# Fifteen activation transposes moved from TensorE to the DMA queue in an eight-core hybrid decoder step

## What is computed

```
h   = rms_norm(x) * (1 + scale1) + shift1          # first norm
p   = h @ W_in                                     # seven column blocks of 512: q, f, i, g, B, C, h
mix = [HGRN2 recurrence over (q, f, i) * silu(g),  B * conv3(C * h)]
x   = x + gate1 * (mix @ W_out)
h2  = rms_norm(x) * (1 + scale2) + shift2          # second norm
x   = x + gate2 * (relu(h2 @ W_up)^2 @ W_down)     # the channel mixer
y   = rms_norm(x) * g_final
```

## Time and profile before

| | us |
|---|---|
| three timed runs | 858.78, 861.19, 865.7 (median 861.19) |
| the profiled execution | 858.85 |
| its span, first to last instruction | 857.3 |
| spans of the eight cores | 854.6 to 857.3 |
| TensorE busy | 810.3 |
| VectorE, ScalarE, POOL busy | 454.1, 369.2, 173.1 |

### The profile page before, as it was taken

One profiled execution on the slowest core, in us unless ns is written; L12 is line 12 of the kernel. 1 busy time (PEld: TensorE's weight loads), 2 busy tenths in 40 slices (PEclk: granted clock), 3 DMA queues, 4 the chain that ended last, 5 costly groups with the idle time before them and its releaser, 6 DMA issues.

```text
span 857.3 us, 16496 instructions; the slowest of 8 cores (854.6 to 857.3 us)
## 1 busy us (share of the span) xinstructions
PE 810.3 (95%) x5917; PEld 512.2 (60%) x5917; DVE 454.1 (53%) x876; ACT 369.2 (43%) x803; POOL 173.1 (20%) x231
## 2 busy tenths in 40 slices
PE   1479999999999999999999999999999999999996
PEld 1348876586876868656545654564456445644864
DVE  2366997377777867953015553455345535541522
ACT  3267963364676778447303322332233213310412
POOL 3110143353324231510003011101110111111002
PEclk9989999999999999999999999999999999999998
DMA  8999935988893349599995325212421432112001
GB/s 151 191 193 189 198 99 95 209 208 175 197 222 129 125 146 153 149 174 192 188 198 184 112 56 160 99 50 62 151 96 50 78 107 75 38 37 99 26 1 50
DMA packets 38957, 109.57 MB, mean 128 GB/s; under 512 B 15030, under 2 KB 16054, under 8 KB 33884
## 3 DMA queue, kind: packets, MB, share of 16 engines
q0 software_dynamic: 6624, 44.14, 31.1%
q1 hardware_dynamic: 30524, 58.34, 22.1%
q10 hardware_dynamic: 1728, 6.03, 2.2%
HBM read 123.93 MB, written 22.68 MB: 171 GB/s over the span
## 4 chain that ended last, share of the span: by engine, by line
PE 83%; DMA 11%; DVE 2%; issue 2%; ACT 1%; POOL 1%; DVEq 0%; ACTq 0%; POOLq 0%; SPq 0%
PE B L510 82%; DMA gates<-xr 4%; DMA win<-w_in 3%; DMA xe<-xp 3%; PE B L521 1%; ACT W L537 1%; DMA xn<-xp 1%; DMA xr<-xs 1%; POOL xr L544 0%; DVE Sd L544 0%; POOL mix L544 0%; DVE W L554 0%; DVE sg L554 0%; DVE ub L544 0%; DVE W L544 0%
## 5 line engine op out<-in xcount | busy, mean ns | idle before, releaser
L510 PE MATMUL B<-h2T,wup 128*128 128x384 bf16 (+1 forms) x1536 | 240.2, 317 | 0.0
L510 PE MATMUL B<-wdn,uT 128*128 128x512 bf16 (+1 forms) x1120 | 235.9, 373 | 0.0
L510 PE MATMUL B<-hT,win 128*128 128x256 bf16 (+1 forms) x1728 | 194.3, 269 | 6.1 <-DMA win<-w_in 5.4
L510 PEld LDWEIGHTS B<-h2T,wup 128*128 128x128 bf16 x1536 | 149.5, 98 | 83.8
L537 ACT ACTIVATE W<-B 128x384 f32<-128x384 f32 (+2 forms) x209 | 103.6, 497 | 204.3 <-PE B L510 187.3
L510 PEld LDWEIGHTS B<-wdn,uT 128*128 128x128 bf16 x1120 | 109.6, 98 | 124.8
L510 PEld LDWEIGHTS B<-hT,win 128*128 128x128 bf16 x1728 | 158.9, 99 | 27.9 <-issue 7.1
L544 POOL TENSOR_TENSOR xr<-xr,W 128x512 f32<-128x512 f32 x63 | 82.3, 1312 | 291.8 <-DVE W L544 256.3
L544 DVE TENSOR_TENSOR uT<-W,B 128x384 bf16<-128x384 f32 (+1 forms) x160 | 83.8, 525 | 80.5 <-ACT W L537 74.8
L544 DVE TENSOR_TENSOR W<-B,Gp 128x512 f32<-128x512 f32 (+1 forms) x65 | 44.2, 680 | 152.9 <-PE B L510 152.7
L537 ACT ACTIVATE W<-xr 128x1024 bf16<-128x1024 f32 (+2 forms) x19 | 18.3, 965 | 131.5 <-POOL xr L544 126.8
(11 more groups left out here) (157 smaller groups left out, 660.9 us busy)
## 6 DMA issues: line engine op xcount, KB each, us to landing
x<-xr SPq DMA_DIRECT2D x17, 512.0 KB, 10.6
xn<-x SPq DMA_DIRECT2D x17, 512.0 KB, 5.8
xr<-x SPq DMA_DIRECT2D x17, 512.0 KB, 4.1
ada<-w_ada POOLq DMA_DIRECT2D x8, 1024.0 KB, 14.7
xr<-xp SPq DMA_DIRECT2D x16, 512.0 KB, 10.0
wup<-w_up POOLq DMA_DIRECT2D x8, 1024.0 KB, 13.7
wdn<-w_down POOLq DMA_DIRECT2D x8, 1024.0 KB, 39.7
yp<-xr SPq DMA_DIRECT2D x15, 512.0 KB, 2.6
```

Source lines behind the costliest of these rows:

```text
L510: ins = e.matmul(o_, lhsT=l_, rhs=r_, start=st, stop=sp_, skip_group_check=True)
```

## The change

Three kinds of block turn from `tr` to `turn`: the first norm of prompt tiles 4 to 7 (two blocks each), both norms of the sample tile (`sample_mod`: its first norm, and its block in group 0), and the second norms of the prompt blocks of groups 0 and 1. That is 8 + 2 + 5 = 15 blocks; prompt tiles 0 to 3 keep TensorE's transposes. In each, scale and shift are then applied in place. The semaphore of a DMA is now keyed by the part of a buffer that it writes as well, so that two transposes into one operand are waited for apart.

```
-            key = eng + ((":in:" + writes[0][0].name) if (writes and (writes[0][0].rng is not None or not reads)) else (":out:" + reads[0][0].name))
+            key = eng + ((":in:" + writes[0][0].name + writes[0][1]) if (writes and (writes[0][0].rng is not None or not reads)) else (":out:" + reads[0][0].name))
...
     def sample_mod(nbv, nbn, dst, dst_n, c0, j_sh, j_sc, spare=None):
-        M, Mn = NR.take()
-        Mb = M[:, :].bitcast(BF16)
-        tr([(Mb[:, j * 128:(j + 1) * 128], nbv[:, j * 128:(j + 1) * 128], ident) for j in range(8)], [nbn, "cB"], [Mn])
+        turn(dst[:, :, c0:c0 + 128], nbv, [nbn], [dst_n + "#d0"], 128 * 2048)
...
-            tt("dve", tmv, trv, scb, ALU.mult, [Mn, "modT%d#%d" % (j_sc // 8, jh)], [Wn])
+            tt("dve", tmv, hv, scb, ALU.mult, [dst_n + "#d0", "modT%d#%d" % (j_sc // 8, jh)], [Wn])
...
     def norm1(kind, ti, eng="act"):
+        if ti >= 4:
+            for b in range(2):
+                turn(h[:, :, b * 128:(b + 1) * 128], nbs[b][0], [nbs[b][1]], ["%s#d%d" % (hn, b)], 128 * 2048)
+            for jj in range(8):
+                ts("dve", h[:, jj, :], h[:, jj, :], modT[:, 8 + jj, 0:1], modT[:, jj, 0:1], ALU.mult, ALU.add,
+                   [hn + "#d0", hn + "#d1", "modT0#%d" % (jj // 4), "modT1#%d" % (jj // 4)], ["%s#%d" % (hn, jj)])
+            return h, hn
...
-                norm2(bgroups[0][n_ - 5:n_ - 4], None, "h2T0_", n_ - 5)
+                norm2(bgroups[0][n_ - 5:n_ - 4], None, "h2T0_", n_ - 5, cross=True)
...
-            norm2(bgroups[1], h2T, "h2T", 0, got)
+            norm2(bgroups[1], h2T, "h2T", 0, got, cross=True)
```

More of the change, by code:

```diff
@@ L879, in sample_mod @@
     def sample_mod(nbv, nbn, dst, dst_n, c0, j_sh, j_sc, spare=None):
-        M, Mn = NR.take()
-        Mb = M[:, :].bitcast(BF16)
-        tr([(Mb[:, j * 128:(j + 1) * 128], nbv[:, j * 128:(j + 1) * 128], ident) for j in range(8)], [nbn, "cB"], [Mn])
+        turn(dst[:, :, c0:c0 + 128], nbv, [nbn], [dst_n + "#d0"], 128 * 2048)
         for jh in range(2):
             W, Wn = (spare[0][:, jh * 512:(jh + 1) * 512], "%s#%d" % (spare[1], jh)) if spare else WT.take()
-            trv = Mb[:, jh * 512:(jh + 1) * 512].rearrange("p (j s t) -> p j s t", s=16, t=8)
             tmv = W[:].rearrange("p (j s t) -> p j s t", s=16, t=8)
@@ L889, in sample_mod @@
             shb = AP(modT, (j_sh + 4 * jh) * 17 + 1, [[544, 128], [17, 4], [1, 16], [0, 8]])
-            tt("dve", tmv, trv, scb, ALU.mult, [Mn, "modT%d#%d" % (j_sc // 8, jh)], [Wn])
-            tt("dve", hv, tmv, shb, ALU.add, [Wn, "modT%d#%d" % (j_sh // 8, jh)], ["%s#%d" % (dst_n, jh)])
+            tt("dve", tmv, hv, scb, ALU.mult, [dst_n + "#d0", "modT%d#%d" % (j_sc // 8, jh)], [Wn])
+            tt("dve", hv, tmv, shb, ALU.add, [Wn, dst_n + "#d0", "modT%d#%d" % (j_sh // 8, jh)], ["%s#%d" % (dst_n, jh)])
     def norm1(kind, ti, eng="act"):
@@ L1226, in norm2 @@
                 hn = pre + "%d" % s
-                turn(dst, nbv, [nbn], [hn], 128 * 2048)
+                turn(dst, nbv, [nbn], [hn + "#d0"], 128 * 2048)
                 for j in range(8):
                     ts("dve", dst[:, j, :], dst[:, j, :], modT[:, 24 + j, 0:1], modT[:, 16 + j, 0:1], ALU.mult, ALU.add,
-                       ["%s#%d" % (hn, j), "modT2#%d" % (j // 4), "modT3#%d" % (j // 4)], ["%s#%d" % (hn, j)])
+                       [hn + "#d0", "modT2#%d" % (j // 4), "modT3#%d" % (j // 4)], ["%s#%d" % (hn, j)])
                 continue
```

## The result

The changed kernel took 900.86, 900.87 and 904.46 us, the kernel before 858.78 to 865.7 in the same series (four executions, median 861.8): ratio of the means 1.0465, 95% interval 1.0404 to 1.0526. It is slower, by 40 us, and outside the predicted range.

The account below looks back on a forecast made before the run. TensorE was taken as the bound, almost without idle time from 130 us on. Terms: -6.7 + 2 + 0.5 + 1.5 = -2.7 us, from a median of 861.19 to 858.5 us; range 852.3 to 873.

Parts of the forecast that it names:

- the price of tile 4's pair: Prompt tile 4: two transposes behind SP's earlier load land late, sm0 waits behind them; TensorE stall 0 to 8 us, taken 2.
- the top of a landing: Transposing DMA beside weights: up to 7.5 us taken, from kS and vS loads; ends kept at 1.3 and 58 us.
- The slower rival: Small packets take single turns beside weights, so stalls reach their upper ends: +13.4 us, 874.6 us; chance 0.21.
- the prediction's estimate: Transposes beside weights: by the skill page's 9 to 17 descriptors a packet, 62 descriptors make 4 to 7 turns, 4 to 7 us.
- the removed 6.7 us: TensorE, fifteen normed blocks: eight transposes each, 0.45 us a block, leave a stretch without slack; -6.7 us.
- zero for w_down and for PSUM: Group 0's `down`: 6.4 us of room covers 3.9 us later weights; PSUM: no wait for a bank shows; both zero.
- the other two stalls: Tile 5's second transpose behind convs: 0 to 3.3 us, taken 0.5; group 1's `up`, third transpose behind Gs: 0 to 8.8, taken 1.5.
- SP's own time: SP's queue: issuing fifteen transposes at 1.26 us, 19 us spread over 270 us of mostly waiting; counted as zero.
- Median landing 4 to 10 us; above 20 us the slower rival holds: Profile test on the first fifteen transposes' landings: median 4 to 10 us expected, above 20 us means packets take single turns.
- The warning on ScalarE's squares: ScalarE's next square into W0 or W1 waits until a transpose has landed; named as a possible unforeseen wait, no size given.

Follow-up runs that it names:

- the first experiment: Changed kernel with prompt tile 4's two blocks back on TensorE's transposes, the other thirteen by DMA; engine lists also reordered: 910.37 us, ratio 1.0628.
- eight quiet blocks: Kernel before, with DMA transposes only for prompt tiles 6 and 7, the sample tile and group 0's second norms: 863.25 us, ratio 1.0041.
- the two kernels that differ by one dependence: Changed kernel, tile 4's pair issued after xr and w_ada 10 land; w_ada 11 held until the pair lands (ratio 1.028) or not held (1.0361).

## Why the prediction was wrong

**The step that failed** is the price of tile 4's pair: "between 208.4 + 2.6 = 211.0 and 208.4 + 15 = 223.4", a stall "between 0 and 8 us; I take 2, since only one weight load is then in flight". The mechanism (VectorE in order, sm0 behind hT0) was right; the term was 0 to 40.1 us by core. On core 1 the second of the pair was issued at 196.17 and landed at 211.6, within that span. On core 4 the pair landed at 228.2 and 256.6, as the chain of waits has it (start, us, what; the second piece is ScalarE's wait for the second transpose):

```profile
197.88 30.28 DMA hT<-W
...
229.53 27.08 another core or an unknown queue
```

Three choices made it. I took 7.5 us from the earlier trace rows, two ordinary loads of 1 KB rows, as the top of a landing although I had named 58 us as the upper end in the same part. I read a term from one core, while the time is the slowest of eight, so a stall with a wide spread counts with its worst value. And "only one weight load is then in flight" asked how many loads run, not which of them starts into the pair. The kernel before had that to read, in POOL's timeline of the same core: w_ada 11 is issued 3 us before the 208.4 at which I had the pair start, and the first load of St 10 us after it.

```profile
191.52 0.59 POOL L574 DMA_DIRECT2D ada<-w_ada  x1
205.68 0.59 POOL L574 DMA_DIRECT2D ada<-w_ada  x1 [0.22 <-issue]
218.90 0.73 POOL L574 DMA_DIRECT2D St<-srec  x1
```

**The slower rival** (packets take single turns, 874.6 us) had the sign and the place, but its price used the same 15 us for the pair. Its rate is right beside w_down, about one small packet for each weight packet: group 1's first two transposes landed after 42 to 68 us on the eight cores. That cost TensorE nothing there, and 22 to 27 us in the first experiment. Tile 4 is another case: 25 packets in 2 us are far fewer, and weights slow down as well. The Trainium skill's "DMA: Bandwidth & Descriptors", section "Queues, rings and completion order", gives typically 9 to 17 descriptors a turn, by the prediction's estimate 4 to 7 us a landing; beside w_down the runs show about one 256-byte packet for each weight packet and 40 to 47 us, and the measurement decides. Whether a turn holds one packet of each queue or several of both, these counts do not tell.

**What held:** the removed 6.7 us, and zero for w_down and for PSUM. **What came out right by luck:** the other two stalls. Tile 5 waited 0.5 us, but not for a transpose behind convs: on core 1 convs landed 5.0 us after its issue, not 31.5, and tile 5's second transpose at 228.5 us, not 255.2 to 261.4. Its last scale and shift steps stood late in VectorE's list. Group 1's `up` waited 1.3 us on every core, but on core 1 its third transpose had landed at 441.5 us, 12 us before `up`; its eight steps stood behind a product with Gp that waited for TensorE. Core 1, tile 5 and then group 1:

```profile
253.93 0.85 DVE L550 TENSOR_SCALAR hT<-hT,modT 128x256 bf16<-128x256 bf16 x3
...
448.89 0.69 DVE L544 TENSOR_TENSOR W<-B,Gp 128x512 f32<-128x512 f32 x1 [9.92 <-PE B L510]
449.50 3.87 DVE L550 TENSOR_SCALAR h2T<-h2T,modT 128x128 bf16<-128x128 bf16 x8
```

SP's own time, priced at 19 us for the fifteen, was 85 to 88 us on cores 1, 4 and 7: on core 1 the issue of one transpose of group 1 alone held SP for 38.8 us.

```profile
388.68 38.81 SPq L570 DMA_TRANSPOSE h2T<-W  x1
```

None of TensorE's waits on core 1 can be traced to it, so the zero stood, but not for the reason given. "Median landing 4 to 10 us; above 20 us the slower rival holds" was a poor test: the median was 4.9 to 9.3 us on all eight cores, since two more late landings of fifteen don't move it. The warning on ScalarE's squares came true without a price here (on core 4 they waited 40.0 us for transposes, beside VectorE's 40.6), and with one in the first experiment (25 us).

**The advice.** The advice of the Trainium skill's "VectorE: DVE Perf Modes", section "Rules for kernel authors", to transpose 128 x 128 on TensorE where PSUM will do holds here for tile 4. For the eight quiet blocks the landings of 3.0 to 7.3 us cost nothing that could be shown, but nothing was gained by leaving it either.

**Open:** why the DMA engines hold each other when a weight load starts into a transpose, and why this differs from the steady stream of w_down. That the meeting is the cause of tile 4's loss is shown (the two kernels that differ by one dependence, the one that holds w_ada 11 alone, and the counts of packets left); how it works inside is not. The Trainium skill's "DMA: Bandwidth & Descriptors" says under "Back-pressure in remote DMA", of transfers between cores, that stalled writes stall the source engine's other queues too; core 4's rows, where weights and transposes both nearly stop, look alike, but no run here shows that it is the cause. That the gain of 3.6 us did not show with eight quiet blocks is explained only in part.

## What to carry to other kernels

In these runs a transposing DMA was cheap where no large load started into it or streamed beside it: look in the list of DMA issues for what starts in the 15 us after it, on any queue. Where a landing has a wide spread, price it at its worst over the cores, together with everything queued behind the instruction that waits for it. A change of a planner's input moves other waits as well; compare every engine's list before a run is read as a test of one edit.

## What the runs showed of the hardware

- A small packet of a transpose took 0.02 us of an engine alone, about 0.66 us beside a running stream of 8192-byte packets, and 1.2 us (25 in 2 us on 16 engines) after a weight load had started into it. In that last state (core 4, 210 to 240 us) both queues together moved 33 to 72 GB/s with a DMA share of 1.02 to 1.77, against 274 on core 1 from 210 to 220 us.
- A pair whose packets met the start of w_ada 11 with 64 or more of its 2048 left took 20 to 56 us to the second landing; with some 20 left it took 14 to 15, and with no weight load beside it 4.0 to 5.3.
- The issue of a transpose took SP 1.26 us where nothing ran beside it, and 38.8 us behind another one beside w_down (core 1).
- TensorE's granted clock on core 4 fell from 1.00 to 0.50 during the wait of 40.1 us; it was 0.60 from 262 to 264 us, the wait having ended at 260.2, and 1.00 again from 264 on.
